# One inference step of a hybrid retention and attention trunk: weights in groups of three at the stage joints, an own x for the first gated tile, tables loaded during the last attention

## The reference, cut to what matters

```
for x in (1024 prompt rows, 64 sample rows):                    # D = 1024
    proj = rmsnorm(x) @ w_in        # rq rk rv rg aq ak av ag iq ik iw
    rq, rk = rope(rq), rope(rk) / sqrt(128)                      # 4 heads of 128
    ro, state = retention(rq, rk, rv, state)                     # chunks of 64, decay gamma^|n-m|
    ro = rmsnorm(ro, per head) * ret_gn_g * silu(rg)
    top = indexer top-k of the admissible keys (iq, ik, iw)
    ao = softmax attention over the chosen keys (8 heads of 64, 2 kv heads) * silu(ag)
    y  = rmsnorm(x + concat(ro, ao) @ w_out) * final_g
```

## Time and profile before

| | us |
|---|---|
| median of three runs (lowest to highest) | 928.48 (925.73 to 930.24) |
| the profiled execution | 923.67 |
| its span, first to last instruction | 922.1 |
| TensorE busy in the span | 803.6 (87%) |
| VectorE, ScalarE, GpSimd busy | 481.7, 334.1, 161.9 |
| mean granted TensorE clock | 0.936 of full speed |

### The profile page before, as it was taken

One profiled execution on the slowest core, in us unless ns is written; L12 is line 12 of the kernel. 1 busy time (PEld: TensorE's weight loads), 2 busy tenths in 40 slices (PEclk: granted clock), 3 DMA queues, 4 the chain that ended last, 5 costly groups with the idle time before them and its releaser, 6 DMA issues.

```text
span 922.1 us, 12271 instructions
## 1 busy us (share of the span) xinstructions
PE 803.6 (87%) x4185; PEld 674.2 (73%) x4185; DVE 481.7 (52%) x1179; ACT 334.1 (36%) x753; POOL 161.9 (18%) x352
## 2 busy tenths in 40 slices
PE   4788988998889899688699799999948999999984
PEld 3677877876768678677677588888837888888873
DVE  5433677778787878879625233333234533333322
ACT  5545555656456665567422111111034300000000
POOL 0323313131302122010022111112212000000000
PEclk9889979799999999799789799999978999999997
DMA  9412021202202020013263211111156433333321
GB/s 275 143 45 89 23 88 31 96 15 93 65 12 70 8 81 5 24 33 104 59 188 98 75 63 63 63 63 63 63 172 217 159 111 111 112 112 111 111 61 57
DMA packets 36462, 79.00 MB, mean 86 GB/s; under 512 B 7280, under 2 KB 9728, under 8 KB 35264
## 3 DMA queue, kind: packets, MB, share of 16 engines
q1 hardware_dynamic: 30112, 59.07, 20.5%
q0 software_dynamic: 6304, 19.36, 6.3%
HBM read 57.88 MB, written 20.53 MB: 85 GB/s over the span
## 4 chain that ended last, share of the span: by engine, by line
PE 54%; DVE 20%; issue 8%; DMA 7%; ACT 5%; POOL 3%; SPq 1%; DVEq 0%; POOLq 0%; ACTq 0%
PE bank L777 41%; DVE probs L1487 4%; DMA xT<-turned_x 3%; PE bank L891 3%; DVE work L1393 2%; DMA stage<-in_w_in 2%; PE bank L791 1%; DVE idx L1374 1%; DVE w_lo L1279 1%; DVE work L1428 1%; PE bank L837 1%; PE bank L880 1%; DVE top L1426 1%; PE bank L838 1%; PE bank L936 1%
## 5 line engine op out<-in xcount | busy, mean ns | idle before, releaser
L777 PE MATMUL bank<-w_hi,xT 128*128 128x512 f32 (+1 forms) x1152 | 379.2, 399 | 17.3 <-DMA xT<-turned_x 9.0
L777 PEld LDWEIGHTS bank<-w_hi,xT 128*128 128x128 f32 x1152 | 221.1, 195 | 68.1 <-DMA xT<-turned_x 12.8
L777 PE MATMUL bank<-w_lo,xT 128*128 128x512 f32 (+1 forms) x576 | 226.9, 394 | 0.0
L777 PEld LDWEIGHTS bank<-w_lo,xT 128*128 128x128 f32 x576 | 112.3, 195 | 19.4
L891 PE MATMUL bank<-v_sb,pT 128*128 128x64 f32 x648 | 91.9, 282 | 11.9 <-ACT pT L1124 11.5
L891 PEld LDWEIGHTS bank<-v_sb,pT 128*128 128x128 f32 x648 | 85.4, 202 | 19.6 <-ACT pT L1124 18.9
L880 PE MATMUL bank<-ident,probs 128*128 128x128 f32 x324 | 56.1, 286 | 17.4 <-ACT probs L1113 17.2
L1374 DVE SCALAR_TENSOR_TENSOR idx<-bank,iw_s,idx 128x384 f32<-128x384 f32 (+5 forms) x93 | 53.5, 611 | 32.3 <-ACT bank L1159 31.4
L1113 ACT ACTIVATE probs<-probs,low 128x128 f32<-128x128 f32 (+8 forms) x68 | 54.6, 803 | 42.1 <-DVE low L1487 42.0
L1124 ACT COPY pT<-bank 128x512 f32<-128x512 f32 (+3 forms) x104 | 48.8, 494 | 39.5 <-PE bank L880 38.6
L777 PE MATMUL bank<-w_hi,mT_hi 128*128 128x512 f32 x144 | 57.5, 399 | 2.6 <-DVE y_row L1663 2.6
(11 more groups left out here) (185 smaller groups left out, 1203.4 us busy)
## 6 DMA issues: line engine op xcount, KB each, us to landing
xT<-turned_x SPq DMA_DIRECT2D x36, 512.0 KB, 4.1
stage<-in_w_in SPq DMA_DIRECT2D x40, 256.0 KB, 3.1
turned_x<-xT SPq DMA_DIRECT2D x9, 1024.0 KB, 5.3
xin<-in_x_prompt SPq DMA_DIRECT2D x16, 256.0 KB, 3.9
early<-in_w_in SPq DMA_DIRECT2D x4, 1024.0 KB, 6.5
y_row<-in_x_prompt SPq DMA_DIRECT2D x16, 256.0 KB, 4.5
stage<-in_w_out SPq DMA_DIRECT2D x16, 256.0 KB, 3.4
out<-y_row POOLq DMA_DIRECT2D x8, 512.0 KB, 2.9
```

The costliest lines, as they stand in the source:

```text
L777: mm = pe.matmul(out, (lo if which == 2 else hi)[:, k, :], (w_lo if which == 1 else w_hi)[slot][:, k, 0:width], start=(i == 0), stop=(i == ...
```

## The change

At the first joint (A to R) ScalarE and VectorE take rg 0 to 2 ahead of tile 0's copies, rg 3 to 5 where 0 to 3 were, and rg 6 and 7 where 4 to 7 were; SyncE loads rg 3 to 5 ahead of x of tile 1. The tables that tile 0 needs (angles, `dec_t`, `start_t`) and `fg_t` are loaded during the last attention, the others after it, and two waits on `ao_stored` go. At the second joint (R to O) the first gated tile gets a buffer of its own, `xT_0`, loaded behind the last x of stage R; ag is loaded, rounded and split in groups of 3, 3 and 2, and x of tile 1 is loaded between them. `output` takes the statistics of each half after its add, rescales and stores by halves, and the sample's x rows go into `gate` instead of `y_row`. Buffers in SBUF are placed anew.

```diff
         def spill_no(phase, t):
-            return t + (TILES if phase == "O" else 0)
-        R_CONSTS = 16 * 5
+            return t + (TILES - 1 if phase == "O" else 0)
+        R_EARLY = 16 * 2
+        R_CONSTS = 16 * 3
...
+            def load_first_gated():
+                sp.wait_ge(ao_stored, AO_STORES)
+                sp.dma_start(xT_0[:].bitcast(F32).rearrange("p a k n -> p a (k n)"), xT_mem[0:P, :, :])\
+                  .then_inc(xT_0_in, 16)
...
+            def load_y_sample():
+                sp.wait_ge(mixed_ready, 2 * TILES)
+                for half in range(2):
+                    sp.dma_start(gate[half * DEC:(half + 1) * DEC, :], xs).then_inc(y_last_in, 16)
...
-            for i in range(item_no["rk", STAGES], item_no["rg", STAGES]):
+            for i in range(item_no["rk", STAGES], item_no["rg", 2 * STAGES]):
                 load(i)
             load_turned("R", 1)
-            for k in range(STAGES, KD):
+            for k in range(2 * STAGES, KD):
                 load(item_no["rg", k])
             with sp.Fori(2, TILES) as t:
                 load_turned("R", t)
-            load_turned("O", 0)
-            for k in range(KD):
+            load_first_gated()
+            for k in range(2 * STAGES):
+                load(item_no["ag", k])
+            load_turned("O", 1)
+            for k in range(2 * STAGES, KD):
                 load(item_no["ag", k])
             load_y(0)
-            for k in range(KD - 1):
-                load(item_no["wo0", k])
-            load_turned("O", 1)
-            load(item_no["wo0", KD - 1])
-            for k in range(KD):
-                load(item_no["wo1", k])
+            for w in ("wo0", "wo1"):
+                for k in range(KD):
+                    load(item_no[w, k])
             load_turned("O", 2)
...
             def gate_r(t, first=False):
-                project("rg", "rg", "O", t, first, x=("spill", spill_no("O", t)))
+                if first:
+                    project("rg", "rg", "O", t, True, x=("first",), of_x=xT_0)
+                else:
+                    project("rg", "rg", "O", t, False, x=("spill", spill_no("O", t)))
...
+            for k in range(3):
+                round_w("rg", k)
             retained(0)
             turned(0)
-            for k in range(4):
+            for k in range(3, 6):
                 round_w("rg", k)
             square(0)
             retained(1)
-            for k in range(4, KD):
+            for k in range(6, KD):
                 round_w("rg", k)
...
             turned(NT - 1)
-            for k in range(4):
+            for k in range(3):
                 round_w("ag", k)
             square(NT - 1)
             retained(SAMPLE)
-            for k in range(4, KD):
+            for k in range(3, 6):
                 round_w("ag", k)
             turned(SAMPLE)
+            for k in range(6, KD):
+                round_w("ag", k)
             for k in range(4):
                 round_w("wo0", k)
...
-            dve.wait_ge(ao_stored, AO_STORES)
             dve.memset(state[:], 0.0).then_inc(state_zero, 1)
+            for k in range(3):
+                split_w("rg", k)
...
             rotate_k(SAMPLE)
-            for k in range(4):
+            for k in range(3):
                 split_w("ag", k)
             retain(NT - 1, state, P)
-            for k in range(4, KD):
+            for k in range(3, 6):
                 split_w("ag", k)
             decay_scores(SAMPLE, dec_s)
+            for k in range(6, KD):
+                split_w("ag", k)
...
-                    dve.tensor_tensor(y_row[:, s], of(key)[:], y_row[:, s], ALU.add).then_inc(*drains(key))
+                    dve.tensor_tensor(row[:, s], of(key)[:], row[:, s], ALU.add).then_inc(*drains(key))
+                    wait_drained(dve, key)
+                    ins = half_stats(row, half_)
+                ins.then_inc(stat_done, 1)
+                mean_square(stat_no("y", t))
+                dve.wait_ge(rstd_ready, power_no("y", t) + 1)
                 for half_ in range(2):
-                    wait_drained(dve, (f"y{half_}", "O", t))
-                mean_square(y_row, stat_no("y", t))
-                dve.wait_ge(rstd_ready, power_no("y", t) + 1)
-                dve.scalar_tensor_tensor(out=y_row[:], in0=y_row[:], scalar=rstd[:, 0:1], in1=fg_t[:],
-                                         op0=ALU.mult, op1=ALU.mult).then_inc(y_ready, 1)
+                    s = slice(half_ * BW, (half_ + 1) * BW)
+                    dve.scalar_tensor_tensor(out=row[:, s], in0=row[:, s], scalar=rstd[:, 0:1], in1=fg_t[:, s],
+                                             op0=ALU.mult, op1=ALU.mult).then_inc(y_ready, 1)
...
-            store_attended(SAMPLE)
-            pool.wait_ge(ao_stored, AO_STORES)
-            for dst, src in ((dec_t, decay), (dec_s, decay_sample), (start_t, from_start)):
-                pool.dma_start(dst[:].rearrange("p h n -> p (h n)"), src).then_inc(r_const_in, 16)
...
+            load_angles(0)
+            for dst, src in ((dec_t, decay), (start_t, from_start)):
+                pool.dma_start(dst[:].rearrange("p h n -> p (h n)"), src).then_inc(r_early_in, 16)
+            pool.dma_start(fg_t[:], fg_row.broadcast_to([P, D])).then_inc(fg_in, 16)
+            store_attended(SAMPLE)
```

More of the change, by code:

```diff
@@ L745, in _ @@
                 load_turned("O", t)
[L746 to L747 removed]
+            load_y(NT - 1)
+            load_y_sample()
         @block.tensor
@@ L783, in product, with project @@
                     mm.then_inc(*fills(key))
-            def project(name, w, phase, t, first, part=(0, PRODUCTS), x=None, last=False):
-                product((name, phase, t), SLOT[w], WIDTH[w], xT_hi, xT_lo, w if first else None, part, x, last)
+            def project(name, w, phase, t, first, part=(0, PRODUCTS), x=None, last=False, of_x=xT):
+                product((name, phase, t), SLOT[w], WIDTH[w], of_x[:, 0], of_x[:, 1], w if first else None, part, x,
+                        last)
             def turn_rows(key, rows, n):
@@ L1284, in _, with half_stats, mean_square @@
             STAT = 4
-            def mean_square(rows, no):
-                for half in range(2):
-                    ins = dve.bn_stats(stats[:, half, :], rows[:, half * BW:(half + 1) * BW])
-                ins.then_inc(stat_done, 1)
+            def half_stats(rows, half):
+                return dve.bn_stats(stats[:, half, :], rows[:, half * BW:(half + 1) * BW])
+            def mean_square(no):
                 parts = stats[:].rearrange("p a (b c) -> p (a b) c", c=3)
@@ L1654, in lo_mixed, with output @@
                        mT_lo[:, s, :].rearrange("p k n -> p (k n)"), mT_hi[:, s, :].rearrange("p k n -> p (k n)"))
-            def output(t):
-                dve.wait_ge(y_in, 32 * (t + 1))
+            def output(t, row=y_row):
+                if row is gate:
+                    dve.wait_ge(y_last_in, 32)
+                else:
+                    dve.wait_ge(y_in, 32 * (t + 1))
                 for half_ in range(2):
@@ L1691, in _ @@
             output(NT - 1)
-            output(SAMPLE)
+            output(SAMPLE, gate)
         @block.gpsimd
@@ L1894, in finish @@
                 power(power_no("y", t), 1)
-                pool.wait_ge(y_ready, t + 1)
-                if isinstance(t, int) and t == SAMPLE:
-                    pool.dma_start(y_sample[0], y_row[0:DEC, :]).then_inc(y_stored, 16)
-                else:
-                    pool.dma_start(y_prompt[0, bass.ds(t * P, P), :], y_row[:]).then_inc(y_stored, 16)
+                for half in range(2):
+                    s = slice(half * BW, (half + 1) * BW)
+                    pool.wait_ge(y_ready, 2 * t + half + 1)
+                    if isinstance(t, int) and t == SAMPLE:
+                        pool.dma_start(y_sample[0, :, s], gate[0:DEC, s]).then_inc(y_stored, 16)
+                    else:
+                        pool.dma_start(y_prompt[0, bass.ds(t * P, P), s], y_row[:, s]).then_inc(y_stored, 16)
             pool.wait_ge(ro_stored, 16 * NT)
```

56 lines of the change are left out of this document (32 added, 24 removed).

## The result

The changed kernel takes 904.41 us (median of four runs, 897.91 to 905.20) where the kernel before took 927.36 beside it (925.73 to 930.24). The medians differ by 23.0 us. 900.0 us and a gain of 28.5 us were forecast; 904.41 is inside the range, but nearer to rival A's 905.8 than to the forecast, so the time alone can't tell the two apart; the traces can. Two later sets with the same kernel gave 24.0 us (0.9764) and 24.5 us (0.9741).

The account below looks back on a forecast made before the run. TensorE was taken as full in the output loop, so time could be won only at the joints; 1.2 + 9.1 + 16.8 + 1.4 = 28.5 us less than the median 928.48 gave 900.0 us, range 895.5 to 907.

Parts of the forecast that it names:

- rival A: Second joint: weight ring becomes the bound, wo0 1 to 3 also take 6.8 us, joint gives 11.0; 905.8 us; chance 0.14.
- Tables, 1.2 us: First joint: early angle and other tables remove TensorE's 1.49 us wait for rotated keys; gain 1.2 us (0.8 to 1.5).
- Weights by threes, 9.1 us: First joint: fewer rg loads ahead of x of tile 2 end the 6.89 us wait; gain 9.1 us (8.5 to 9.6).
- with the loop's 7.1: First joint, tile 2: end of v to end of q falls from 16.2 us to the loop's 7.1, giving 9.1.
- Rival B: First joint: x of tile 2 still late behind rg6 and rg7, so 9.1 is not won; 909.1 us; chance 0.05.
- Second joint, 16.8 us: R to O: early ag and xT_0; at most 19.1 us won, less 2.3 waiting for SiLU: 16.8 (14.4 to 18.5).
- wo0 0 is issued about 675.4: Second joint: wo0 0 issued behind the y rows, lands at 682.2 after 6.8 us; rg's bank free at 689.9.
- The low reading by the taking of turns: Second joint: with the state store earlier, wo0 0's transfer is shorter; wait falls to 0.6 us and time to 898.3.
- rival D: Output loop: half stores of y_row hold SyncE's queue, seven tiles stretch by 4.7 us each; 933 us; chance 0.02.
- The end, 1.4 us: After TensorE's end: last store issued 0.86 us earlier and 0.5 shorter at 128 KB; gain 1.4 us (0.8 to 1.8).
- The clock after 2.60 us: Last 48 matmuls: the 2.60 us wait stays; behind it they took 12.8 us for 11.2, 1.6 lost.
- Rival C: Whole change: only the chain's transfers (angles, y reload) are removed, 2.6 us; 925.9 us; chance 0.03.

Follow-up runs that it names:

- rg alone: The kernel before with only rg loaded, rounded and split by threes; 920.65 us, ratio 0.9959 to the kernel before.
- the tables late: The changed kernel with the tables and angles of tile 0 issued after the sample's attended rows, as before; 906.74 us, ratio 0.9765.
- after: Profile of the changed kernel in its first set: profiled execution 904.78 us; median of four runs 904.41 us, ratio 0.9734 to the kernel before.
- k1: The changed kernel, unedited, measured again in the second later set; 901.79 us, ratio 0.9741 to the kernel before.
- k0: The changed kernel, unedited, measured again in the first later set; 901.59 us, ratio 0.9764 to the kernel before.
- the end undone: The changed kernel with one store, one rescaling and the reload of y_row, as before; 899.48 us, ratio 0.9708.
- all three together: The changed kernel with SiLU ahead of wo0, tile 7's first add ahead of the low part, and 101 met waits at TensorE's start; 895.48 us, ratio 0.9645.
- the SiLU kernel: The changed kernel with rg's first SiLU ahead of wo0 0 to 3, VectorE's sample retention ahead of their splits; 900.45 us (0.9725), then 900.21 (0.9709).
- the kernel with SiLU and add first: The SiLU kernel plus VectorE's add of tile 7's first output half ahead of splitting the sample's mixed rows; 897.34 us, ratio 0.9676.

## Why the prediction was right, and where it was off

**Tables, 1.2 us: right, alone and in company.** The keys of tile 0 are turned without a wait, and the gain was 1.2 to 1.4. The step took each edit's price from the trace of before, though, where the angles were nearly in time. With weights by threes beside them they are not (2.32 and 1.52 us in the kernel with rg alone, 3.0 us with the tables late), so the early tables also protect 3 us that the prediction had booked under the weights. Half of that is the lower clock behind two waits close together, which no term held.

**Weights by threes, 9.1 us: mechanism right, size off by the x of tile 2.** The five issues are two, the queue is free, and the two halves of x are issued at 510.62 and when v ends. The step that failed is "with the loop's 7.1": it assumed the transfer of the loop, 3.6 to 3.9 us, where 5.46 (after) and 4.76 (k1) were measured, because a packet of the program moves beside it. k0, where that packet came before the data of x, gave 9.2. The sign "no wait of over 1 us at tile 2's q" failed in two of the three; the granted 1.00 there held. Rival B had this as a late issue at 909.1; the issue was not late.

**Second joint, 16.8 us: mechanism right, the last term mis-sized.** Turned rows, scores and the ag product came as written, with no wait, and the least of 22.1 us was reached (22.3) once the SiLU stood first. The wait for the SiLU was put at 2.3 us without a fall of the clock; it was 3.41, 3.82 and 2.87, and the clock fell in two of the three, so the term was 13.6, 13.2 and 15.7. Of the 3.2 us that after fell short of 16.8, 1.8 are that clock, which the prediction kept for its range. 1.1 are the longer wait, and 0.2 the work itself (22.3 for 22.1). The step that failed for the wait is "wo0 0 is issued about 675.4", which is 3.5 us after the end of v; it was 4.87, 4.67 and 4.66 (673.15 in after). ag5 was split by 671.88, but the two issues of y rows in front took 1.4 to 1.6 us of SyncE's queue. From there on the sum held almost to the digit: the transfer took 6.8, 7.3 and 6.6 us, the load of wo0 3 2.5, 2.6 and 2.4 for "load 2.6", and from wo0 0's landing to the free bank in after are 7.71 us for 1.45 + 2.6 + 3.67 = 7.72. Rival A had wo0 1 to 3 at 6.8 us each; wo0 1 did take 5.2 and wo0 2 4.5, while all transfers together moved 263 GB/s, but the bank hangs on wo0 3, which was as quick as behind an empty queue. So A's mechanism did not come, though its loss of clock did. The low reading by the taking of turns, a wait of 0.6 and 898.3, did not come: its condition, the queues apart, was not met, with 71.0% of the engines' time on SyncE's queue and 30.5% on GpSimd's while wo0 0 moved. That the order of ScalarE and VectorE makes the wait is shown: with the SiLU first it is gone at a DMA share of 0.82, no lower than the 0.78 of k1.

**The ring later on: right.** wo1 7 was split 39.8 us after the end of v (708.05 in after), 2.7 later than forecast and still in time. The stretch behind the joint is 182.74 against 182.75 us, so rival D (stores that stretch the output loop) is refuted, and so is the y half of A.

**The end, 1.4 us: three quarters of it did not come.** The last issue is 4.63 us after the last matmul instead of 5.28: 0.65, where 0.86 were forecast. The statistics end 0.8 us sooner, as written, but from the start of the rescaling to the last issue are 1.74 us instead of 1.58, since the second store is issued behind the first. The store of half size landed in 2.5 us instead of 2.9, 0.4 instead of 0.5 (by the Trainium skill, "DMA: Bandwidth & Descriptors", section "Anatomy of one DMA", 2.0 us and 128 KB would be an estimated 2.3; the profile has 2.3 to 2.5). But from the last landing to the end of the span there are 6.1 us instead of 5.4, and what is left is 0.35 (0.32 to 0.39 in the three profiles). The prediction took that piece as fixed; this is the step that failed. Both values come again, 5.4 to 5.5 with one store (rg alone, the end undone) and 6.1 in k0, k1 and all three together. No row says what it is; it stays open. That the reload cost nothing was right: it landed with the last product in before and in the kernel with the end undone.

**The clock after 2.60 us.** It was said to cost 1.6 and to stay. In 10 of the 12 profiles with that wait the last 48 matmuls took 12.7 to 12.9 us, in two (after and the second run of the SiLU kernel) 11.3: the same kernel, the same wait, no fall. The 1.5 us that after shows there are no gain of the change; they are luck, and hide part of the 3.8 us that it lost in stage A.

**Rival C** (2.6 us, 925.9) fell with the two large terms; undoing the second joint alone costs 12.9 us in the profile.

**The one thing not in any step** is stage A. In the profiles stage R starts between 468.16 and 475.04 us. The two kernels built on before start it at 468.6 and 468.7; of the twelve profiles on the changed kernel one is at 468.2 and eleven are at 470.1 to 475.0, the latest with the tables late. One profile of each can't tell a cost of the change in stage A from the spread. The clock granted there moves: 390 to 470 had 0.91 in before and 0.86 in after (0.84 in k0, 0.87 in k1), while 100 to 200 had 0.86 in before and 0.91 in after. The two rows:

```profile
390.00:470.00 80.00, 62.92 (x409) 54.68 (x409) 60.37 (x143) 50.54 (x91) 6.57 (x18) 0.91 0.25 75
```
```profile
390.00:470.00 80.00, 62.67 (x393) 54.67 (x391) 57.31 (x138) 47.55 (x86) 8.39 (x22) 0.86 0.27 84
```

The same shows between runs: of after, one took 897.91 at a mean granted clock of 0.959, the other three 904.05 to 905.20 at 0.941 to 0.944. Whether the moved code or the new places have a part in stage A is open (the early tables hardly, since the kernel without them starts stage R last): the two SiLU kernels lost 3 us there twice, the two with the add did not (470.58 and 470.32). It is the likely place of the 3 to 4 us that the SiLU edit won in its profile and not in its time, but that was not separated.

## What to carry to other kernels

At a joint between stages look first at what each engine's hand-written order puts ahead of the step that the busiest engine waits for; here ScalarE's roundings ahead of one SiLU cost 3 to 5 us in the profile, which a change of order took away there, though hardly in the times. When a sum hangs on one late transfer, count the issues that stand before it in its queue, and follow the one block that the busiest engine's release waits for, not the ones around it. Edits at one joint are not additive: loads moved ahead delay what the other edit meant to have early, so measure them together and apart.

## What had not been expected of the hardware

- A packet of 0.02 MB on the queue that the profile calls instruction took one DMA engine's time for 0.9 to 1.9 us. Where it began with the data of a 512 KB load (ten profiles), the load took 4.8 to 5.5 us instead of 3.7; where it began 1 us sooner (k0) or 5.5 us before the issue (two kernels), 3.7. In straight-line code around the joints these packets came 24 to 38 us apart, and none came in the loop of stage R or, in after, in the output loop. 101 fulfilled waits ahead moved it off the load in both kernels that had them.
- The same wait of 2.60 us took the last 48 matmuls to 12.8 us in ten profiles and left them at 11.3 in two; at the SiLU it cost 1.7 to 1.8 us after waits of 2.46, 3.39, 3.41 and 3.82 us, and only 0.3 and 0.4 after 2.87 (k1) and 3.68 (tables late). At x of tile 2 nothing was lost after 2.01 (after), but 1.4 us after 1.86 (the kernel with SiLU and add first). A wait of 1.49 us with none close before it left the clock up in the three profiles that have it; one of 1.52 right behind one of 0.73 or 2.32 did not. So between 1.5 and 3.8 us the length of the wait alone did not decide.
- From the last landing to the end of the span are 5.4 us with one store of 256 KB and 6.1 with two of 128 KB.
